# A hybrid decoder step: decode joined to the linear chain, the value product in four parts, 520 finishing columns

## The reference

```python
def mla_keys(c, kr, w_uk, g_kn):
    k_nope = jnp.einsum('bsr,rhd->bshd', c, w_uk)      # 8 heads of 64 from a latent of 256
    ...
    return rms_norm(jnp.concatenate([k_nope, k_rope], axis=-1), g_kn)
...
s = block_scores(c, kr)            # q . normed keys, for each page
p = jnp.exp(s - m_new[..., None])  # softmax over the pages, in one pass
acc = alpha * acc + jnp.einsum('bhqk,bkr->bhqr', p, c)
...
lat = acc / l[..., None]
return jnp.einsum('bhqr,rhd->bqhd', lat, w_uv)
```

## Time and profile before

| | |
|---|---|
| median of 3 runs | 1620.64 us (1620.57 to 1622.29) |
| profiled execution | 1616.67 us, its span 1614.7 |
| mean granted clock of TensorE | 0.95 |
| PE / DVE / ACT / POOL busy | 92 / 49 / 37 / 18% |
| last page matmul of the decode starts | 703.49 us |
| first linear tile | 726.24 us |

### The profile page before, as it was taken

One profiled execution on the slowest core, in us unless ns is written; L12 is line 12 of the kernel. 1 busy time (PEld: TensorE's weight loads), 2 busy tenths in 40 slices (PEclk: granted clock), 3 DMA queues, 4 the chain that ended last, 5 costly groups with the idle time before them and its releaser, 6 DMA issues. The chain is left out here.

```text
span 1614.7 us, 34170 instructions
## 1 busy us (share of the span) xinstructions
PE 1484.0 (92%) x11404; PEld 1386.1 (86%) x11404; DVE 792.0 (49%) x1494; ACT 599.6 (37%) x1487; POOL 293.8 (18%) x481
## 2 busy tenths in 40 slices
PE   7858979999999999969999998869999999999998
PEld 6746659998899899859999995549998999999998
DVE  5664544655664664542334336754455433334444
ACT  3334435655555556531122224322222331133211
POOL 2250005554544454420000000000040000000000
PEclk9978988999999999989999998879999999999999
DMA  5002126555555555512223214423222222222222
GB/s 208 17 10 56 41 84 179 163 155 148 164 151 148 159 159 147 157 38 92 91 92 127 84 55 136 134 92 104 96 78 74 83 91 81 88 92 91 81 103 79
DMA packets 118943, 170.64 MB, mean 106 GB/s; under 512 B 25457, under 2 KB 96146, under 8 KB 118034
## 3 DMA queue, kind: packets, MB, share of 16 engines
q1 hardware_dynamic: 118866, 169.56, 33.4%
HBM read 153.20 MB, written 7.53 MB: 100 GB/s over the span
## 5 line engine op out<-in xcount | busy, mean ns | idle before, releaser
L968 PE MATMUL ps<-wq_hi,ct_hi 128*128 128x260 f32 x1024 | 303.0, 296 | 18.3 <-ACT s_nope L773 11.3
L968 PE MATMUL ps<-wq_lo,ct_hi 128*128 128x260 f32 x1024 | 292.0, 285 | 0.0
L968 PE MATMUL ps<-wq_hi,ct_lo 128*128 128x260 f32 x1024 | 292.0, 285 | 0.0
L1212 PE MATMUL ps<-x_hi,ring_hi 128*128 128x268 f32 x1280 | 266.2, 289 | 11.2 <-DVE ring_lo L1175 9.7
L858 DVE TENSOR_REDUCE k_sums<-k_squares 128x8 f32<-128x512 f32 (+1 forms) x256 | 172.9, 684 | 200.5 <-ACT k_squares L772 200.3
L1212 PE MATMUL ps<-x_lo,ring_hi 128*128 128x268 f32 x1280 | 263.8, 288 | 0.0
L1212 PE MATMUL ps<-x_hi,ring_lo 128*128 128x268 f32 x1280 | 263.3, 287 | 0.0
L716 POOL TENSOR_TENSOR ct_lo<-ct_raw,ct_hi 128x256 fp32r<-128x256 f32 x256 | 189.0, 739 | 355.1 <-ACT ct_hi L765 353.7
L1149 ACT ACTIVATE ring_hi<-ring_raw 128x1024 fp32r<-128x1024 f32 x126 | 129.0, 1024 | 271.0 <-PE ps L1212 229.2
L772 ACT ACTIVATE k_squares<-ps 128x512 f32<-128x512 f32 x256 | 153.0, 598 | 191.8 <-PE ps L968 171.3
L968 PEld LDWEIGHTS ps<-wq_hi,ct_hi 128*128 128x128 f32 x1024 | 195.7, 191 | 22.9 <-issue 22.7
(11 more groups left out here) (291 smaller groups left out, 2131.8 us busy)
## 6 DMA issues: line engine op xcount, KB each, us to landing
ct_raw<-in_ct SPq DMA_DIRECT2D x256, 144.0 KB, 2.3
c_values<-in_c SPq DMA_DIRECT2D x256, 128.0 KB, 2.4
ring_raw<-in_wmain SPq DMA_DIRECT2D x40, 512.0 KB, 3.2
ring_raw<-in_up SPq DMA_DIRECT2D x32, 512.0 KB, 3.2
ring_raw<-in_down SPq DMA_DIRECT2D x32, 512.0 KB, 3.3
state_new<-in_state SPq DMA_DIRECT2D x4, 1024.0 KB
out_st_s<-state_new SPq DMA_DIRECT2D x4, 1024.0 KB, 4.5
ring_raw<-in_reto SPq DMA_DIRECT2D x8, 512.0 KB, 3.3
```

The costliest lines, as they stand in the source:

```text
L968: mm = nc.tensor.matmul(k_ps[j % 2][:, f, 0:WQN], ch[:, j, r * P:(r + 1) * P], w[:, x2, r, f, :], start=(r == 0 and x == 0), stop=(r == 1 ...
L1212: mm = nc.tensor.matmul(ps[s][:, b, 0:HT], w[:, k, :], x[:, k, b * HT:(b + 1) * HT], start=(k == 0 and j == 0), stop=(k == nk - 1 and j == 2))
```

## The change

1. The decode and the projection of the retention stand in one block: the last sequence's closing on PE lies between the first eight tiles, maximum behind tile (0,1), spread (1,0), value product (2,0), finish (3,0), output (3,1). The first ring splits go ahead of the last two groups of the decode.
2. The value pages have one buffer of 32. SP loads value groups of a sequence as: 0 in its group 6, 1 and 2 in its group 7, then 3, 4, 5 and (6, 7) in groups 0 to 3 of the next. `keys()` and `values()` each look up their own numbers.
3. PE's loop runs over one sequence, seven times; the half of the query weights is addressed by a register.
4. The steps of the norm stand one by one behind the eight sums of groups 0 and 1, and every step of the closing one group later. The raw scores get a second buffer for it.
5. The value product's 32 matmuls are four times 8, behind the four pages of group 4.
6. From linear tile 16 on, the 16 learned tokens are left out: two halves of 260 columns in place of 268, also in what empties the sums, in gates and in the output.

The diff, cut:

```diff
+FT = T - N_META
+HF = FT // 2
...
+def rsqrt_step(dve, i, y, t, tmp, chain, at, done):
+
+    if i == 0:
+        dve.tensor_scalar(y.bitcast(I32), t.bitcast(I32), -0.5, float(0x5F3759DF), ALU.mult, ALU.add).then_inc(chain, 1)
+        return
+    dve.wait_ge(chain, at + i)
+    if i % 3 == 1:
+        dve.scalar_tensor_tensor(tmp, y, -0.5, y, ALU.mult, ALU.mult).then_inc(chain, 1)
+    elif i % 3 == 2:
+        dve.tensor_tensor(tmp, tmp, t, ALU.mult).then_inc(chain, 1)
+    else:
+        dve.scalar_tensor_tensor(y, tmp, 1.5, y, ALU.add, ALU.mult).then_inc(done if i == 9 else chain, 1)
...
-    cv = p("c_values", [P, 2, NPG, KVL + 1])
...
+    EARLIER, OWN = {0: (3,), 1: (4,), 2: (5,), 3: (6, 7)}, {6: (0,), 7: (1, 2)}
...
-            def keys(n, half, pages, first=False):
-
+            def keys(n, half, first=False):
+                pages = table_row(n)
...
-            def values(b, g, pages):
-
+            def values(b, g):
+                pages = table_row(NGR * b + g)
+                if g == 0 and not isinstance(b, int):
+                    sp.wait_ge(pv_done, b + 1)
                 for j in range(GP):
-                    page = cv[:, bass.ds(b % 2, 1), GP * g + j, 0:KVL] if isinstance(g, int) else \
-                        cv[:, bass.ds(b % 2, 1), bass.ds(GP * g + j, 1), 0:KVL].rearrange("p o g r -> p (o g) r")
-                    sp.dma_start(page, m.d_c[bass.ds(pages[j], 1)].rearrange("o k r -> k o r")).then_inc(cv_in, 16)
+                    sp.dma_start(cv[:, GP * g + j:GP * g + j + 1, 0:KVL], m.d_c[bass.ds(pages[j], 1)].rearrange("o k r -> k o r")).then_inc(cv_in, 16)
 
             for g in range(NGR):
-                pages = table_row(g)
-                keys(g, g % 2, pages, first=g < 2)
-                values(0, g, pages)
-            sp.wait_ge(zeroed, 9)
-            sp.wait_ge(ab_done, 1)
+                keys(g, g % 2, first=g < 2)
+                for v in OWN.get(g, ()):
+                    values(0, v)
             with sp.Fori(1, NB) as b:
                 for g in range(NGR):
-                    pages = table_row(NGR * b + g)
-                    keys(NGR * b + g, g % 2, pages)
-                    if g == 0:
-                        sp.wait_ge(cv_in, 16 * NPG * b)
-                        sp.wait_ge(pv_done, 1 * b)
-                    values(b, g, pages)
+                    keys(NGR * b + g, g % 2)
+                    for v in EARLIER.get(g, ()):
+                        values(b - 1, v)
+                    for v in OWN.get(g, ()):
+                        values(b, v)
+            for g in EARLIER:
+                for v in EARLIER[g]:
+                    values(NB - 1, v)
+            sp.wait_ge(kr_sq, NB * NGR)
+            sp.dma_start(uvr[:], m.d_uv).then_inc(uv_in, 16)
+            chain.sync(sp)
...
-                    if closes and g == 2 and j == 3:
+                    if closes and (g, j) == (3, 3):
                         exp(b - 1)
-                    if closes and g == 4 and j == 0:
+                    if closes and (g, j) == (5, 0):
...
-            exp(b)
...
+            chain.scalar(act, close)
...
-                    normalize(b - 1)
+                    norms(b - 1)
                 for j in range(GP):
                     sums(n, g, j)
-                    if closes and (g, j) == (1, 2):
+                    if closes and g < 2:
+                        refine(b - 1, *((0, 1), (2,), (3,), (4,), (5,), (6,), (7,), (8, 9))[GP * g + j])
+                    if closes and (g, j) == (2, 0):
+                        normalize(b - 1)
+                    if closes and (g, j) == (2, 1):
+                        max_of_keys(b - 1)
+                    if closes and (g, j) == (2, 3):
                         max_of_heads(b - 1)
-                    if closes and (g, j) == (2, 2):
+                    if closes and (g, j) == (3, 2):
                         less_max(b - 1)
-                    if closes and (g, j) == (4, 1):
+                    if closes and (g, j) == (5, 1):
                         l_parts(b - 1)
-                    if closes and (g, j) == (4, 3):
+                    if closes and (g, j) == (5, 3):
...
-            def page(n, x2, j, first=False):
+            def page(n, b, j, first=False):
...
-                            mm = nc.tensor.matmul(k_ps[j % 2][:, f, 0:WQN], ch[:, j, r * P:(r + 1) * P], w[:, x2, r, f, :],
+                            mm = nc.tensor.matmul(k_ps[j % 2][:, f, 0:WQN], ch[:, j, r * P:(r + 1) * P], of_sequence(w, b)[:, r, f, :],
...
-            def values(b, half):
-
-                pe.wait_ge(ones_set, 3)
+            def values(b, first=0, end=NGR):
+
+                pe.wait_ge(ones_set, 2)
                 pe.wait_ge(p_done, b + 1)
                 pe.wait_ge(cv_in, 16 * NPG * (b + 1))
-                for g in range(NGR):
+                for g in range(first, end):
                     for j in range(GP):
-                        nc.tensor.matmul(acc_ps[32 * j:32 * j + 32, 0:KVL + 1], pall[:, GP * g + j, :], cv[:, half, GP * g + j, :],
+                        nc.tensor.matmul(acc_ps[32 * j:32 * j + 32, 0:KVL + 1], pall[:, GP * g + j, :], cv[:, GP * g + j, :],
                                          start=(g == 0), stop=False, skip_group_check=True)
-                pe.wait_ge(set_in, 80)
+                if end < NGR:
+                    return
...
-                    if closes and (g, j) == (1, 2):
+                    if closes and (g, j) == (2, 2):
                         turn_max(b - 1)
-                    if closes and (g, j) == (2, 2):
+                    if closes and (g, j) == (3, 2):
                         spread_max(b - 1)
-                    if closes and (g, j) == (3, 2):
-                        values(b - 1, 1 - x2)
-                    if closes and (g, j) == (4, 2):
+                    if closes and g == 4:
+                        values(b - 1, 2 * j, 2 * j + 2)
+                    if closes and (g, j) == (5, 2):
                         finish(b - 1)
...
-            with pe.Fori(0, NB // 2 - 1) as twice:
-                for x2 in (1, 0):
-                    for g in range(NGR):
-                        group(2 * twice + 2 - x2, x2, g, g % 2, closes=True)
+                    group(0, 2 * pair + half, half)
+            with pe.Fori(1, NB) as b:
+                for g in range(NGR):
+                    group(b, g, g % 2, closes=True)
             b = NB - 1
-            for g in range(NGR):
-                group(b, 1, g, g % 2, closes=True)
-            turn_max(b)
-            spread_max(b)
-            values(b, 1)
-            finish(b)
-            pe.wait_ge(lat_done, NB + 1)
-            for h in range(MH):
-                for r in range(2):
-                    mm = nc.tensor.matmul(acc_ps[64 * (h % 2):64 * (h % 2) + VD, (h // 2) * NB:(h // 2 + 1) * NB],
-                                          uvr[:, r, h * VD:(h + 1) * VD], lat[:, r, :, h], start=(r == 0), stop=(r == 1),
-                                          skip_group_check=True)
-            mm.then_inc(o_done, 1)
+
+            def close(i, s):
+                if (i, s) == (0, 1):
+                    turn_max(b)
+                if (i, s) == (1, 0):
+                    spread_max(b)
+                if (i, s) == (2, 0):
+                    values(b)
+                if (i, s) == (3, 0):
+                    finish(b)
+                if (i, s) == (3, 1):
+                    output()
+
+            def output():
+                pe.wait_ge(lat_done, NB + 1)
+                pe.wait_ge(uv_in, 16)
+                for h in range(MH):
+                    for r in range(2):
+                        mm = nc.tensor.matmul(acc_ps[64 * (h % 2):64 * (h % 2) + VD, (h // 2) * NB:(h // 2 + 1) * NB],
+                                              uvr[:, r, h * VD:(h + 1) * VD], lat[:, r, :, h], start=(r == 0), stop=(r == 1),
+                                              skip_group_check=True)
+                mm.then_inc(o_done, 1)
+
+            chain.tensor(pe, (k_free, NPG * NB), close)
...
+    def tensor(self, pe, before=None, more=None):
+        nc, ring, ps = self.nc, self.ring, self.ps
+
+        def pair(stage, i, before=None):
+            for s in range(2):
+                pe.wait_ge(ring.lo_done, ring.base + 2 * i + s + 1)
+
+                if before and i == 0:
+                    pe.wait_ge(before[0], before[1] + s - 1)
+                elif not isinstance(i, int) or i > 0:
+                    pe.wait_ge(ring.emptied, ring.emptied_base + 2 * i + s - 1)
+                xh, xl = stage.rhs(pe, i, s)
+                nk, skip, half = stage.blocks[s], stage.skip, (T - stage.skip) // 2
+                for k in range(nk):
+                    for j, (w, x) in enumerate(((ring.hi[s], xh), (ring.hi[s], xl), (ring.lo[s], xh))):
+                        for b in range(2):
+                            mm = nc.tensor.matmul(ps[s][:, b, 0:half], w[:, k, :], x[:, k, skip + b * half:skip + (b + 1) * half],
```

(113 more changed lines are left out.)

386 lines of the change are left out of this document (182 added, 204 removed).

## The result

The changed kernel takes 1660.57 us (median of 4 runs, 1656.71 to 1663.40) where the kernel before takes 1620.61: a ratio of 1.0249, 95% interval 1.0220 to 1.0278. Slower was forecast, by 10 us; it is 40, above the range. The profiled executions took 1656.71 and 1616.67, so they differ by 40.0 too.

The account below looks back on a forecast made before the run. PE, busy 92% of the span, bounded the kernel before; SP's lookups would stall it. +34 - 23.9 + 7.9 + 6.9 - 15.6 = +9.3 on 1616.67 gives 1626.0, plus 4.0 to the median: 1630, range 1596 to 1650.

Parts of the forecast that it names:

- PE stands some 6 us once in each sequence, in front of page (3,3): Decode: PE waits for SP's late keys of group 4, so a sequence takes 62.2 us.
- +34 us: Decode's seven closing sequences: +29.5 for the longer cycle and +4.6 for lost clock, bounds +23 and +40.
- Eleven batches follow ... 39.2, until 45.4: SP's queue after keys 7: seven value batches at 3.58 us and four key batches at 3.54, lookups included.
- With that behind half of the stalls, +4.6: Decode: 12 matmuls at half clock lose 1.3 us behind a stall, counted for half of the stalls.
- the product in four parts take 5.76 + 0.5 + 4.15: Group 4 on PE: four pages, their turning and rope, and the value product, 10.4 us, ending at 62.2.
- the 29.5 of the forecast: Decode: seven sequences, each 4.2 us longer at 62.2 us, before any lost clock.
- -15.6: Finishing stages: 260 columns in place of 268 save 3.0 ns on 5184 matmuls, bounds -11 and -20.
- -23.9 + 7.9 + 6.9: Tail: gap and half clock gone -23.9, closing products among tiles +7.9, tile 2's wait and clock +6.9.
- SP keeps up: Rival, chance 0.08: a lookup under 0.87 us on the path, PE bounds, -49.5, 1571 us.
- Register addresses: Rival, chance 0.09: pages addressed by a register cost 150 ns a matmul on PE, +31, 1652 us.
- the same, with branches: Rival, chance 0.05: SP keeps up, but six branches of PE's loop stall 2.9 us each, +17.4, 1588 us.
- SP late by half: Rival, chance 0.12: a lookup of 1.15 us gives 58.8 us a sequence, -19 in all, 1602 us.

Follow-up runs that it names:

- the moved loop: The changed kernel with 40 idle semaphore increments on SP ahead of its loop, which begins 40 instructions later: 1639.48 us (ratio 1.0131).
- the written-out run: The changed kernel with SP's seven turns of the decode written one behind another in place of a loop: 1638.45 us (ratio 1.0120).
- the filled stall: The changed kernel with 32 unused matmuls behind page (3,2) of each closing sequence, to keep PE running: 1644.31 us (ratio 1.0152).
- the two kernels without range checks: The changed kernel, lookups without range check: value product in four parts 1569.68 us, in one run behind page (4,2) 1563.31 us.

## Why the prediction was right or wrong

**Right: the mechanism.** SP's lookups take SP from an engine that waits to the one that sets the cycle, and PE stalls before page (3,3) for group 4's keys. Taking the check away (91 us) shows it from one side, the unchanged time of the kernel before without checks from the other. The place of that stall and its releaser are as told. That the single norm steps are covered fits, since PE shows no wait for the norm, but it was not tried in this kernel. PE's branches had nothing to cover, at 0.21 us.

**Wrong: one stall.** "PE stands some 6 us once in each sequence, in front of page (3,3)" was forecast. There are two: 3.2 to 4.2 us there, and 2.9 to 3.2 ahead of page (7,3), for the keys behind the end of SP's loop. Together they come near the 6 told, but the second has its cause in the branch that the forecast left out.

**Wrong: the size of the decode.** +34 us was forecast; the first linear matmul comes at 777.28 where the last page's slot ended at 703.61 before, +73.7. Of this 1.4 had come before the seven sequences began (at 299.18 in place of 297.75), and 72.3 in them. The steps that failed:

- "Eleven batches follow ... 39.2, until 45.4". This counts SP's cycle as if it had no loop: the end of the loop was put at nothing, without a reason. I weighed a slow branch as a rival for PE alone, whose branch turned out to take 0.21 us, and not for SP, whose body grew from 277 to 353 instructions and lay where it is fetched anew in each turn. From the branch to the next instruction there are 2.5 to 2.7 us. Worth 21 us by the moved loop (the written-out run's 22 have shorter lookups in them), 18 by its gap, which is 3.0 shorter in each of six turns.
- "With that behind half of the stalls, +4.6". The half clock came behind all seven and for 14 to 20 matmuls each, not 12, and pages (3,3) and (4,0) both stand on the cycle: 13 to 16 us by the filled stall, against 4.6.
- "the product in four parts take 5.76 + 0.5 + 4.15". The 4.15 is of one run. In parts it is 1.0 more (the two kernels without range checks): 7 us, though one run in the changed kernel gave back only 2 to 5. I had set the parts' price as the later end alone, "one page, 1.4 us"; the run moved back showed that the later end costs next to nothing, since keys 7 wait for squares behind it.

With the 29.5 of the forecast, 29.5 + 21 + 16 + 7 = 73.5 by the medians, against the 72.3 measured in the seven sequences. That it fits so well is in part luck: each term is good to a few us and was taken by itself, and by the traces the sum is 29.5 + 18 + 13 + 7 = 67.5, which leaves some 5 us without a cause.

**Wrong: the columns.** -15.6 was forecast; -24.0 was measured by the run with all columns and -24.8 by the two profiles from tile 16 on, outside my bound of -20. The step that failed took 260 columns from a page of the decode. In the finishing stages such a matmul takes 0.1185, not 0.1200; why the pages are slower by 1.5 ns was not tried.

**Right: the tail.** -23.9 + 7.9 + 6.9 = -9.1 was forecast, and the profiles show -8.9 from the last page to tile 16; 73.7 - 8.9 - 24.8 are the 40.0. Tile 2 waits 5.61. The 5.6 told holds a slip (35.1 + 1.05 + 1.29 is 37.4, not 37.6), so that it agrees to the hundredth is luck. Without range checks, where tile 2 does not wait, the same stretch is 101.8 us, 17.2 less than before, near the -23.9 + 7.9 = -16.0 of the forecast.

**The rivals.** "SP keeps up" is true as a condition: with cheap lookups 1569.7 for 1571. "Register addresses" and "the same, with branches" are out: with SP out of the way PE's pages run at full clock in 57.0 us a sequence, and the branch of PE's new loop took 0.21 us: that its body of 547 instructions would stall like the one of 1070 was wrong. "SP late by half" is out too: a checked lookup cost what was told, with gaps of 1.63 to 1.66 us where SP waits for nothing.

## What to carry to other kernels

When a change gives the queueing engine more to do, write its whole cycle down, from the release of a buffer to the next, with its lookups, their range checks and its own branch; mean load (57 of 58 us here) says nothing. Look at the branch of every engine's loop, not only of the engine that bounds, by the gap between the rows on its two sides; if a loop that grew is slow there, try moving it before rewriting it. And price a stall of TensorE with the half clock behind it, on each page that the next release waits for.

## What was not expected of the hardware

- From the branch of a loop of 353 instructions on SP to the next instruction there were 0.25 to 0.32 us where the loop begins at SP's instruction 235 or 363, and 2.5 to 3.1 where it begins at 323, with five packets of 8 KB fetched in each turn.
- A lookup of four page numbers with range checks leaves a gap of 1.66 us between transfers, one without 0.61. The load itself is some 300 ns of it in both (298 and 301).
- 40 idle instructions made a kernel 21 us faster, and 32 idle matmuls in each of seven sequences one 16 us faster (13 of them seen in the trace).
